# Two slots instead of three for the split weight tiles of the FFN phase of a streaming encoder step

## What is computed

```python
x = x + mixed @ p['w_out']
h = rmsnorm(x, p['norm_ffn'])
gate, ffn_new = causal_dwconv(h @ p['w_gate'], ffn_past, p['ffn_conv_w'], p['ffn_conv_b'])
x = x + (jax.nn.silu(gate) * (h @ p['w_up'])) @ p['w_down']
```

## Time and profile before

| | |
|---|---|
| median of 3 runs | 2757.32 us (2754.12 to 2764.69) |
| profiled execution | 2763.85 us, of it the span of the trace 2762.1 us |
| mean granted TensorE clock | 0.952 of full |
| TensorE matmul busy | 2478.7 us, 90% of the span |
| TensorE weight load busy | 2201.1 us, 80% |
| GpSimd busy | 1188.0 us, 43%; 888.8 us of it the 380 subtractions of L1969, mean 2.34 us |
| DVE busy | 1161.0 us, 42% |
| ScalarE busy | 970.0 us, 35%; 391.6 us of it the 380 casts of L1978, mean 1.03 us |
| DMA | 265.52 MB, mean 96 GB/s |
| chain that ended last | TensorE 62% of the span, DMA 2%, DVE 1% |

### The profile page before, as it was taken

How to read it: one execution, slowest core, us unless ns; L and a number is a source line. 1 busy time by engine, 2 the same in 40 slices (tenths; PEclk the granted TensorE clock), 3 DMA queues, 4 the chain that set the end, 5 groups by cost and what they waited for, 6 DMA issues and landing times.

```text
span 2762.1 us, 36172 instructions
## 1 busy us (share of the span) xinstructions
PE 2478.7 (90%) x13445; PEld 2201.1 (80%) x13445; DVE 1161.0 (42%) x1999; ACT 970.0 (35%) x1605; POOL 1188.0 (43%) x616
## 2 busy tenths in 40 slices
PE   5888764688899669999999989999999999999996
PEld 5888752334555369999999988999999999999996
DVE  1297797915895643322433223322233231232221
ACT  4332312014555334333433323433334232343431
POOL 2333249001452035555545535444545444555552
PEclk9999986888999789999999999999999999999998
DMA  4333220020002445444543374533335433344446
GB/s 91 101 100 82 79 43 6 0 1 15 0 0 24 147 115 150 129 122 121 155 148 111 115 84 132 160 107 101 113 94 162 130 103 105 112 124 139 125 125 75
DMA packets 543308, 265.52 MB, mean 96 GB/s; under 512 B 113318, under 2 KB 536906, under 8 KB 543178
## 3 DMA queue, kind: packets, MB, share of 16 engines
q1 hardware_dynamic: 523610, 263.69, 34.9%
q10 hardware_dynamic: 19568, 0.08, 1.3%
HBM read 246.36 MB, written 17.43 MB: 96 GB/s over the span
## 4 chain that ended last, share of the span: by engine, by line
PE 62%; DMA 2%; DVE 1%; SPq 0%; POOL 0%; ACT 0%; issue 0%; ACTq 0%
PE ffn_bank L142 20%; PE ffn_bank L143 20%; PE ffn_bank L144 20%; DMA ffn_w_raw<-in_w_out 1%; DMA ffn_w_raw<-in_w_down 1%; PE ffn_bank L2356 1%; PE ffn_bank L2269 0%; POOL ffn_w_lo L1969 0%; DVE ffn_xm_lo L2102 0%; SPq L1884 0%; ACT ffn_w_hi L1978 0%; PE ffn_bank L2290 0%; DVE ffn_xT L2114 0%; DVE ffn_bank L2135 0%; DVE ffn_yrow L2185 0%
## 5 line engine op out<-in xcount | busy, mean ns | idle before, releaser
L1969 POOL TENSOR_TENSOR ffn_w_lo<-ffn_w_raw,ffn_w_hi 128x1024 fp32r<-128x1024 f32 (+1 forms) x380 | 888.8, 2341 | 897.6 <-ACT ffn_w_hi L1978 897.5
L142 PE MATMUL ffn_bank<-ffn_xf_hi,ffn_w_hi 128*128 128x386 f32 (+5 forms) x1760 | 625.7, 356 | 5.7 <-DVE ffn_xf_lo L2166 5.7
L143 PE MATMUL ffn_bank<-ffn_xf_lo,ffn_w_hi 128*128 128x386 f32 (+5 forms) x1760 | 622.9, 354 | 0.0
L144 PE MATMUL ffn_bank<-ffn_xf_hi,ffn_w_lo 128*128 128x386 f32 (+5 forms) x1760 | 621.7, 353 | 0.0
L1978 ACT ACTIVATE ffn_w_hi<-ffn_w_raw 128x1024 fp32r<-128x1024 f32 (+1 forms) x380 | 391.6, 1033 | 624.7 <-PE ffn_bank L144 343.0
L142 PEld LDWEIGHTS ffn_bank<-ffn_xf_hi,ffn_w_hi 128*128 128x128 f32 x1760 | 331.6, 188 | 20.8 <-issue 6.3
L143 PEld LDWEIGHTS ffn_bank<-ffn_xf_lo,ffn_w_hi 128*128 128x128 f32 x1760 | 332.7, 189 | 12.4
L144 PEld LDWEIGHTS ffn_bank<-ffn_xf_hi,ffn_w_lo 128*128 128x128 f32 x1760 | 332.3, 189 | 12.2
L142 PE MATMUL ffn_bank<-ffn_h_hi,ffn_w_hi 128*128 128x384 f32 (+2 forms) x880 | 312.5, 355 | 21.0 <-POOL ffn_w_lo L1969 17.4
L144 PE MATMUL ffn_bank<-ffn_h_hi,ffn_w_lo 128*128 128x384 f32 (+2 forms) x880 | 310.5, 353 | 0.0
L143 PE MATMUL ffn_bank<-ffn_h_lo,ffn_w_hi 128*128 128x384 f32 (+2 forms) x880 | 310.1, 352 | 0.0
(11 more groups left out here) (346 smaller groups left out, 3488.2 us busy)
## 6 DMA issues: line engine op xcount, KB each, us to landing
ffn_w_raw<-in_w_gate SPq DMA_DIRECT2D x220, 256.0 KB, 3.3
ffn_w_raw<-in_w_up SPq DMA_DIRECT2D x220, 256.0 KB, 3.2
ffn_w_raw<-in_w_down SPq DMA_DIRECT2D x160, 256.0 KB, 3.3
pin_w_raw<-in_w_in SPq DMA_DIRECT2D x96, 256.0 KB, 3.2
ffn_w_raw<-in_w_out SPq DMA_DIRECT2D x160, 128.0 KB, 2.8
ffn_w_raw<-in_w_down SPq DMA_DIRECT2D x80, 192.0 KB, 2.7
mixed<-z_t SPq DMA_DIRECT2D x40, 208.0 KB, 3.1
pin_x<-in_x_prompt SPq DMA_DIRECT2D x4, 2048.0 KB
```

The source lines that it names most:

```text
L142: pe.matmul(out, w_hi, x_hi, start=first, stop=False)
L143: pe.matmul(out, w_hi, x_lo, start=False, stop=False)
L144: return pe.matmul(out, w_lo, x_hi, start=False, stop=last)
L1969: pool.tensor_tensor(w_lo[n % 3][:, 0:c], w_raw[n % 2][:, 0:c], w_hi[n % 3][:, 0:c].bitcast(F32), ALU.subtract).then_inc(s_lo, 1)
```

## The change

`w_hi` and `w_lo` get two slots each instead of three. `after(n)` casts tile n+2 instead of n+3, still once tile n is used. In the head `hi(2)` goes; tile 2 is cast by `after(0)`, behind the square of the first `w_out` tile. The ring of raw tiles, the loads and all other orders stay.

```diff
-        w_hi = [m.sb(f"w_hi{i}", [P, KD * P], F32R) for i in range(3)]
-        w_lo = [m.sb(f"w_lo{i}", [P, KD * P], F32R) for i in range(3)]
+        w_hi = [m.sb(f"w_hi{i}", [P, KD * P], F32R) for i in range(2)]
+        w_lo = [m.sb(f"w_lo{i}", [P, KD * P], F32R) for i in range(2)]
...
-                pool.tensor_tensor(w_lo[n % 3][:, 0:c], w_raw[n % 2][:, 0:c], w_hi[n % 3][:, 0:c].bitcast(F32), ALU.subtract).then_inc(s_lo, 1)
+                pool.tensor_tensor(w_lo[n % 2][:, 0:c], w_raw[n % 2][:, 0:c], w_hi[n % 2][:, 0:c].bitcast(F32), ALU.subtract).then_inc(s_lo, 1)
...
             def hi(n):
-                if n >= 3:
-                    act.wait_ge(s_used, n - 2)
+                if n >= 2:
+                    act.wait_ge(s_used, n - 1)
                 act.wait_ge(s_raw[n % 2], raw_total[n])
                 c = unit_cols(n)
-                act.activation(w_hi[n % 3][:, 0:c], w_raw[n % 2][:, 0:c], ACT.Copy).then_inc(s_hi, 1)
+                act.activation(w_hi[n % 2][:, 0:c], w_raw[n % 2][:, 0:c], ACT.Copy).then_inc(s_hi, 1)
 
             def after(n):
 
-                if n + 3 < UNITS:
-                    hi(n + 3)
+                if n + 2 < UNITS:
+                    hi(n + 2)
...
-            for n in range(3):
+            for n in range(2):
                 hi(n)
                 mixed_hi(0, n)
+            mixed_hi(0, 2)
             mixed_hi(0, 3)
```

More of the change, by code:

```diff
@@ L2282, in make_out @@
                     at = slice(k * P, (k + 1) * P)
-                    ins = three_passes(pe, out_b[o % 2][:, 0:nb], w_hi[n % 3][:, at], w_lo[n % 3][:, at], xm_hi[:, k, 0:nb], xm_lo[:, k, 0:nb],
+                    ins = three_passes(pe, out_b[o % 2][:, 0:nb], w_hi[n % 2][:, at], w_lo[n % 2][:, at], xm_hi[:, k, 0:nb], xm_lo[:, k, 0:nb],
                                        k == 0, k == KD - 1)
@@ L2309, in gate_up @@
                         at = slice(k * P, (k + 1) * P)
-                        ins = three_passes(pe, bk[:, 0:nb], w_hi[n % 3][:, at], w_lo[n % 3][:, at],
+                        ins = three_passes(pe, bk[:, 0:nb], w_hi[n % 2][:, at], w_lo[n % 2][:, at],
                                            xf_hi[:, k, c0:c0 + nb], xf_lo[:, k, c0:c0 + nb], k == 0, k == KD - 1)
@@ L2329, in down @@
                     at = slice(i * P, (i + 1) * P)
-                    ins = three_passes(pe, down_b[o % 3][:, 0:fw], w_hi[n % 3][:, at], w_lo[n % 3][:, at], h_hi[:, i, 0:fw], h_lo[:, i, 0:fw],
+                    ins = three_passes(pe, down_b[o % 3][:, 0:fw], w_hi[n % 2][:, at], w_lo[n % 2][:, at], h_hi[:, i, 0:fw], h_lo[:, i, 0:fw],
                                        i == 0, i == FG[g] - 1)
```

## The result

| | before | after |
|---|---|---|
| median | 2758.53 us (2754.12 to 2764.69, 4 runs) | 2841.55 us (2836.88 to 2842.50, 4 runs) |
| ratio, 95% interval | | 1.0296 [1.0273, 1.0319] |
| profiled execution, span | 2763.85, 2762.1 us | 2836.88, 2835.1 us |
| mean granted clock | 0.952 | 0.951 |
| TensorE matmul busy | 2478.7 us, 90% | 2505.9 us, 88% |

What follows compares the result with a forecast made beforehand. TensorE, busy throughout the FFN phase, was taken as the bound, so late weight tiles lengthen the span. Terms 7.8 + 33 + 6 + 12 + 8 - 3 + 3 + 17 = 84 us gave 2841 us, range 2816 to 2872.

Steps and rivals of the forecast that it cites:

- Down pair: Before down tile 2 in groups 0 and 1 of five blocks: ten stalls of 3.3 us, 33 us.
- Clock: After each of the ten down-pair stalls: 3.4 us at half clock, losing 1.7 us of matmuls each, 17 us.
- Rival A: The clock holds through the short gaps, leaving stalls alone: 67 us slower, 2824 us; chance 0.15.
- Gates: Gate tiles in blocks 0, 1 and 4 begin about 0.21 us late, 37 times: 7.8 us.
- w_out: Every second `w_out` tile late, 0.66 us each in the 384-column blocks: 6 us in all.
- Norm: Last down group beside the next block's norm: every second tile 1.46 us late, eight times, 12 us.
- State writes: Conv-state writes after blocks 1 and 4, one cast tile less in hand: 4.9 and 3.2 us, 8 us.
- Head: Start of the FFN phase: tile 2's cast moves behind the first square, a gain; net -3 us, between 0 and -6.
- DMA lateness: Raw loads issued a tile later, with x, mixer and store DMAs between: 3 us, bounds 0 and 20.
- rival B: Raw loads sharing the queue reach their casts late: 15 us more and a few clock drops, 2860 us; chance 0.18.
- C: Two slots are enough, gate and up tiles covering cast plus subtraction; nothing measurable, 2757 us; chance 0.03.
- D: Faster: ScalarE stops waiting for raw tiles, at the phase's start, up to 8.2 us; 2749 us; chance 0.02.

Runs made afterwards that it cites:

- run 1: Same run as two_plain: the changed kernel with down tiles 0 and 1 one after the other; 2789.38 us, 1.0126 of before.
- run 6: Same run as two_half_pair: the changed kernel with down tile 0 finished when tile 1 is half way; 2804.98 us, 1.0185 of before.
- hi2_lo3: The changed kernel with three slots for the lower halves, two for the upper; 2838.36 us, 1.0311 of before.
- two_castfirst: The changed kernel with the cast ahead of `a` and the square, and `norm_hi` one tile later; 2814.86 us, 1.0213 of before.
- two_turned: The changed kernel with the conv state written once, after block 4, as rows of 512-byte pieces; 2806.51 us, 1.0187 of before.
- two_plain: The changed kernel with down tiles 0 and 1 one after the other instead of interleaved; 2789.38 us, 1.0126 of before.
- two_half_pair: The changed kernel with down tile 0 finished when tile 1 is half way; 2804.98 us, 1.0185 of before.
- run 10: three_head with the conv state written once, after block 4, as rows of 512-byte pieces; 2717.40 us, 0.9865 of before.
- run 11: Same run as two_turned: the changed kernel with the conv state written as rows of 512-byte pieces; 2806.51 us, 1.0187 of before.
- three_head: The kernel before, three slots, with only the cast of tile 2 moved behind the mixer pieces at the head; 2749.16 us, 0.9978 of before.
- two_all_turned: The changed kernel with the edits of two_plain and two_castfirst and the conv state written as rows; 2727.54 us, 0.9898 of before.

## Why the prediction was right, point by point

**What bounds the kernel.** Right. TensorE had no slack in the phase, so every late tile showed in the span: 78.3 us by the traces, 83 by the medians, 84 forecast. TensorE's waits for the lower half came to the 70 to 80 us named as a sign, but in 34 gaps and not in 60 and more: the gate tiles' 0.2 us show no releaser.

**Down pair.** Right in mechanism and size: ten stalls of 3.13 to 3.20 us against 3.28. Runs 1 and 6 tied it to the release of tile 0.

**Clock.** Near in sum, coarse in detail. The step "the ten down-pair stalls are longer than both gaps: 17 us" took a fall for certain after each. It came after seven: tile 2 lost 1.65 to 1.68 us at five places, as the 1.7 of the prediction, 2.7 to 2.8 at two, and 0.1 at three (block 2 group 0, block 3 group 1, block 4 group 0). 14.6 us is the ten stages' 46.2 less their 31.6 of stalls. A full clock behind such gaps was named as a sign of being wrong, and three of ten places show it. Which places fall is not fixed: with the same ten gaps the clock fell after seven in hi2_lo3, after eight in two_castfirst and after all ten in two_turned, and the ten down stages less their stalls lost 13.9 us in the first and 18.1 in the last. So 17 lies within what these traces show, and "2.4 us too dear" is true of one of them. Rival A (no fall, 2824) is wrong by two_plain, whose stages fell by the whole 46 us and not by 32. Leaving out the norm stalls was right: none of the eight was followed by a fall.

**Gates.** Places right, the size 0.29 instead of 0.21 a pair: the sum counted the late start and not that the first matmul behind a gap takes longer to hand over. 37 pairs would make 10.7; the stages show 11.1.

**w_out and norm.** `w_out` 6.3 for 6. Norm: the row of block 1 was said to be near the middle, 1.46; the two gaps there put tiles off by 1.34 and 1.58, with 1.53 and 1.49 in block 0 and 1.06 to 0.94 in blocks 2 and 3, 9.9 us in all. The other 4.6 the sum did not have: mostly the same lateness where the group hands over to the next block's first gate tile (1.1 us for block 1, 2.1 for block 2), and slower first matmuls.

**State writes.** The sum of 8.4 for 8 hides a wrong split: 7.7 us after block 1 and 0.6 at the end, where 4.9 and 3.2 were forecast. The stage after block 1 was 2.5 to 5.7 us shorter in hi2_lo3, two_plain and two_half_pair, which don't touch it, so a single trace doesn't fix this term, and runs 10 and 11 don't either. The forecast's picture of one tile of lead less, 4.9 us after block 1, is neither shown nor refuted.

**Head.** The step that failed. "Net -3, between 0 and -6" was -8.2, outside its bounds, shown once more by three_head alone (-8.3). On the clock of the trace of after, 5.3 us ahead of the one before, the first mixer piece reached its cast at 967.77, which is 973.1 there, as the step had it; its partner at 970.89, 976.2 there, 0.8 us or more ahead of "977 to 979". The step gave each lower half 1.7 to 2.5 us; DVE took 0.96. And it took the half clock of tile 1 as lost anyway, where behind the shorter wait the clock was at full. All three were choices on the careful side.

**DMA lateness, rival B.** Wrong as a cost: the cast's waits for raw `w_gate` fell to 5.7 us, and no gap outside the state writes is put down to a load. That fits the wider spacing, the argument against B, though no run took the spacing alone. The 3 us too many, the stalls of the pair (1.4) and the clock (2.4) too dear, and the head's 5.2 not given made 12 us; gates, norm and the rest gave 6 back. The forecast was close in part by such cancelling, and the medians' 83 is nearer to it than the traces' 78 by the spread of the runs: that part is luck.

**Rivals C and D.** C fell with the down pair, as argued, and not with the gates, though those too were 0.21 us short of covered. The Trainium skill's advice to double-buffer (Trainium Kernel Development and Optimization, Best Practices) speaks of DMA overlapping compute, and the ring that the DMA fills has two slots in both kernels; read for the split halves too, it holds here only where release and need are a whole tile apart: two_all_turned makes them so, and two slots are then 0.4% from three. D's place and size were right (8.2 us), and its gain was outweighed.

## What to carry to other kernels

Judge a ring not by its slots but by the time from the release of a slot to the need of its next content, at each place of the order: a pair of tiles finished together releases the first late, and cost 46 of the 78 us here. Put the instruction that refills a slot ahead of everything in its queue that can wait. And look at small scattered writes: four writes in pieces of 512 bytes, in place of 4-byte ones, gave 1.2%, more than the third slot was worth once the orders were mended (0.4%), though less than the 3.0% that it is worth in the orders as they were.

## What was not expected of the hardware

- Equal gaps of TensorE, 2.96 to 3.05 us of idle, were followed by the half clock at seven places and not at three, and in two_turned at all ten. In two_half_pair none of the ten idles of 1.17 to 1.50 us was, in the changed kernel none of the eight norm gaps nor the idle of 1.88 us ahead of block 2's first gate tile; yet at that last place two_half_pair's clock fell behind 1.84 us, and one idle of 1.53 us was followed by it in the earlier trace rows. The level after a gap is not a function of its length alone; what decides it stays open.
- DVE's subtraction of 128 x 768 took 0.96 us where GpSimd was idle and 2.55 us where GpSimd's subtraction of a weight tile ran beside it (rows at 968.64 and 964.89; GpSimd's, at 964.20, ended 0.81 us before DVE's). The Trainium skill (GPSIMD Engine Reference, Specifications) says that GpSimd shares its SBUF interfaces with VectorE, with contention for a DVE instruction of two SBUF inputs; the two durations agree.
- A write of 0.5 KB in 4-byte pieces took 7.5 us to land, and with such writes beside them the 256 KB loads of `w_up` took 7.9 us instead of 3.3.
